# Head norm jobs at an even pace, their squares split in two parts, silu moved behind the z reload

## The reference, cut to what matters

```python
proj = xn @ w_in
gq = _l2norm(qkv[..., :GDN_WIDTH].reshape(B, L, GDN_HEADS, GDN_DK)) * (GDN_DK ** -0.5)
gk = _l2norm(qkv[..., GDN_WIDTH:2 * GDN_WIDTH].reshape(B, L, GDN_HEADS, GDN_DK))
z = proj[..., COL_GDN_Z:COL_GDN_B].reshape(B, L, GDN_HEADS, GDN_DV)
o_g = (_rmsnorm(o_g.astype(x.dtype), gdn_out_norm_g) * jax.nn.silu(z)).reshape(B, L, GDN_WIDTH)
dq = _rmsnorm(d[..., :DIFF_WIDTH].reshape(B, L, DIFF_HEADS, 2, DIFF_DQK), diff_q_norm_g)
dk = _rmsnorm(d[..., DIFF_WIDTH:2 * DIFF_WIDTH].reshape(B, L, DIFF_HEADS, 2, DIFF_DQK), diff_k_norm_g)
```

## Time and profile before

| what | us |
|---|---|
| median of 3 runs | 1883.97 (1883.55 to 1886.48) |
| the profiled execution, its own time | 1885.86 |
| its span, first to last instruction | 1884.3 |
| TensorE's matmuls, busy | 1728.3 (92%) |
| DVE, ACT, POOL, busy | 1018.8 (54%), 523.7 (28%), 248.3 (13%) |

### The profile page before, as it was taken

How to read it: one execution, slowest core, us unless ns; L and a number is a source line. 1 busy time by engine, 2 the same in 40 slices (tenths; PEclk the granted TensorE clock), 3 DMA queues, 4 the chain that set the end, 5 groups by cost and what they waited for, 6 DMA issues and landing times. The chain is left out here.

```text
span 1884.3 us, 28461 instructions
## 1 busy us (share of the span) xinstructions
PE 1728.3 (92%) x11078; PEld 1617.5 (86%) x11078; DVE 1018.8 (54%) x1469; ACT 523.7 (28%) x781; POOL 248.3 (13%) x434
## 2 busy tenths in 40 slices
PE   5999998897999999874768999999999999999998
PEld 5999977796888888752338999999999999999997
DVE  4444399942565556422263455555555655655654
ACT  4243332211344334301232232212212212212213
POOL 3100022203333333103100000000000000000000
PEclk9999999999899999956868999999999999999999
DMA  4311101022000000017422112101101101101103
GB/s 136 124 45 47 45 24 34 23 97 98 1 10 3 13 1 1 7 45 248 187 107 73 50 60 64 57 22 56 56 22 56 56 22 56 56 22 56 56 0 101
DMA packets 114550, 105.29 MB, mean 56 GB/s; under 512 B 5387, under 2 KB 104221, under 8 KB 112022
## 3 DMA queue, kind: packets, MB, share of 16 engines
q1 hardware_dynamic: 111666, 93.35, 16.0%
q0 software_dynamic: 1536, 8.39, 1.1%
q10 hardware_dynamic: 1270, 2.48, 0.4%
HBM read 86.13 MB, written 18.07 MB: 55 GB/s over the span
## 5 line engine op out<-in xcount | busy, mean ns | idle before, releaser
L2645 PE MATMUL f_up<-h_hi,w_hi 128*128 128x352 f32 x1032 | 335.1, 325 | 1.9 <-DVE w_lo L2454 1.2
L2645 PE MATMUL f_up<-h_hi,w_lo 128*128 128x352 f32 x1032 | 333.4, 323 | 0.0
L2645 PE MATMUL f_up<-h_lo,w_hi 128*128 128x352 f32 x1032 | 333.4, 323 | 0.0
L179 PE MATMUL proj<-x_hi,win_hi 128*128 128x352 f32 x672 | 227.5, 339 | 5.3 <-issue 3.0
L179 PE MATMUL proj<-x_hi,win_lo 128*128 128x352 f32 x672 | 217.9, 324 | 0.0
L179 PE MATMUL proj<-x_lo,win_hi 128*128 128x352 f32 x672 | 217.7, 324 | 0.0
L2645 PEld LDWEIGHTS f_up<-h_hi,w_hi 128*128 128x128 f32 x1032 | 193.8, 188 | 2.5 <-DVE w_lo L2454 1.5
L2645 PEld LDWEIGHTS f_up<-h_hi,w_lo 128*128 128x128 f32 x1032 | 194.1, 188 | 0.0
L2645 PEld LDWEIGHTS f_up<-h_lo,w_hi 128*128 128x128 f32 x1032 | 193.7, 188 | 0.0
L2652 PE MATMUL f_down<-f_g_hi,dn_hi 128*128 128x352 f32 x512 | 165.3, 323 | 0.0
L2652 PE MATMUL f_down<-f_g_hi,dn_lo 128*128 128x352 f32 x512 | 164.7, 322 | 0.0
(11 more groups left out here) (403 smaller groups left out, 3039.3 us busy)
## 6 DMA issues: line engine op xcount, KB each, us to landing
w_raw<-in_w_up SPq DMA_DIRECT2D x44, 512.0 KB, 3.9
win_raw<-in_w_in SPq DMA_DIRECT2D x28, 512.0 KB, 4.0
dn_raw<-in_w_down SPq DMA_DIRECT2D x11, 1024.0 KB, 5.2
p_key<-in_cache_k SPq DMA_DIRECT2D x32, 256.0 KB, 6.6
p_val<-in_cache_v POOLq DMA_DIRECT2D x32, 256.0 KB, 6.8
x_scratch<-feat SPq DMA_DIRECT2D x1, 4224.0 KB, 12.8
feat<-x_scratch SPq DMA_DIRECT2D x1, 4224.0 KB, 18.3
feat<-in_x_prompt SPq DMA_DIRECT2D x8, 512.0 KB, 9.0
```

Of the source, the lines that this page charges most:

```text
L179: mm = nc.tensor.matmul(out, w[:, k, :], x[:, k, g * TG:(g + 1) * TG], start=(k == 0 and i == 0), stop=(k == KT - 1 and i == 2))
L2645: mm = nc.tensor.matmul(up[u % RING][:, 0:TG], a[s][:, kk, :], b, start=(kk + x == 0), stop=(kk == KT - 1 and x == 2))
```

## The change

- Order of tiles: k, v, q, z (K0 = 12, V0 = 16, Q0 = 20, Z0 = 24). Order of jobs: delta-net q, attention k, delta-net k, attention q.
- The 48 jobs are spread over the 40 places from (14, 0) to (27, 0): one at each place, two at every fifth. Two stand at (15, 1), (17, 0), (18, 2), (20, 1), (22, 0), (23, 2), (25, 1) and (27, 0).
- The rows pieces start at (20, 1): two at each place to (21, 1), then one at (21, 2), none at (22, 0), and one at each place to (25, 0). ACT copies them out instead of DVE; they have two buffers, not three; SP stores the pieces of a tile between two weight loads. `bank` and `bank_is_free` give each use the other bank, and make it wait for the use before the last.
- The squares are split for fp32r: ACT rounds them (sq_hi), POOL makes the remainder (sq_lo, in the place of the squares), PE sums both with ones in fp32r: two passes of fp32r in place of one matmul in fp32.
- z goes to memory as it is, by two buffers. In head_gate ACT first waits for z and takes silu of its four tiles, then does what it did.
- The three tail turns stand all in tile 13, and small tensors share memory.

```diff
     def column(n):
+        if n < V0:
+            return COL_DIFF + GW + (n - K0) * P
         if n < Q0:
-            return COL_DIFF + GW + (n - K0) * P
-        if n < V0:
+            return COL_DIFF + 2 * GW + (n - V0) * P
+        if n < Z0:
             return COL_DIFF + (n - Q0) * P
...
     def jobs_in(n, g):
 
-        k = 3 * (n - K0 - 2) + g - 1
-        return range(max(0, 2 * k), min(NJ, 2 * k + 2))
+        k = NG * (n - K0 - 2) + g
+        return range(max(0, k * NJ // 40), max(0, min(NJ, (k + 1) * NJ // 40)))
 
     def pieces_in(n, g):
 
-        k = 3 * (n - Z0) + g
-        if k < 0:
-            return range(0)
-        first = 2 * k if k < 7 else 14 + (k - 7)
-        return range(first, min(NPIECE, first + (2 if k < 7 else 1)))
...
+        k = NG * (n - Q0) + g
+        if 1 <= k < 6:
+            return range(2 * k - 2, min(NT + 1, 2 * k))
+        if 7 <= k < NT + 8:
+            return range(NT + k - 6, NT + k - 5)
+        return range(0)
...
+    def bank_is_free(pe, kind, x):
+
+        u = uses.index((kind, x)) - 2
+        if u < 0:
+            pe.wait_ge(tail_rows, u + 4)
+        elif uses[u][0] == "job":
+            pe.wait_ge(sq_rooted, uses[u][1] + 1)
+        else:
+            pe.wait_ge(tok_kept, uses[u][1] + 1)
...
+                if n >= Q0 + 2:
+                    for g in range(NG):
+                        for p in pieces_in(n - 2, g):
+                            store_rows(sp, p)
...
+            def square_low(j):
+                pool.wait_ge(sq_hi_done, j + 1)
+                nc.gpsimd.tensor_tensor(sq_lo[j % 2][:, :], sq[j % 2][:, :], r32(sq_hi[j % 2][:, :]), ALU.subtract).then_inc(sq_lo_done, 1)
+
+            square(0)
             for j in range(NJ):
-                square(j)
+                if j + 1 < NJ:
+                    square(j + 1)
+                square_low(j)
...
+            def high_square(j):
+                act.wait_ge(sq_made, j + 1)
+                if j >= 2:
+                    act.wait_ge(sq_summed, j - 1)
+                nc.scalar.copy(sq_hi[j % 2][:, :], sq[j % 2][:, :]).then_inc(sq_hi_done, 1)
...
-                    nc.scalar.activation(z_buf[:, :].rearrange("p (g t) -> p g t", g=NG), psum[s][:, :, 0:TG],
-                                         ACT.Silu).then_inc(evacuated, 1)
...
+                    nc.scalar.copy(acc[s][:, 0:T].rearrange("p (g t) -> p g t", g=NG), psum[s][:, :, 0:TG]).then_inc(evacuated, 1)
...
                     for j in jobs_in(*at):
                         if j == 0:
                             act.wait_ge(eps_put, 2)
+                            high_square(0)
+                        if j + 1 < NJ:
+                            high_square(j + 1)
                         square_root(j)
+                    for p in pieces_in(*at):
+                        keep_rows(p)
...
-                pe.wait_ge(sq_made, j + 1)
-                nc.tensor.matmul(small[:, (j + 1) % 2, 0:TG], head_ones[:, e, :], sq[j % 2][:, :], start=True, stop=True
-                                 ).then_inc(sq_summed, 1)
+                bank_is_free(pe, "job", j)
+                pe.wait_ge(sq_lo_done, j + 1)
+                at = small[:, bank("job", j), 0:TG]
+                nc.tensor.matmul(at, head_ones[:, e, :], sq_hi[j % 2][:, :], start=True, stop=False)
+                nc.tensor.matmul(at, head_ones[:, e, :], sq_lo[j % 2][:, :], start=False, stop=True).then_inc(sq_summed, 1)
...
         @block.scalar
         def _(act):
+            act.wait_ge(z_in, 16)
+            for t in range(H):
+                nc.scalar.activation(zT[:, t, :], zT[:, t, :], ACT.Silu).then_inc(z_made, 1)
             n_act(act)
...
-            dve.wait_ge(z_in, 16)
+            dve.wait_ge(z_made, H)
```

More of the change, by code:

```diff
@@ L198, in norm_and_projection @@
     ba_w = m.sb("ba_w", [P, KT, 4 * H], F32R)
-    NTOK = 3
+    NTOK = 2
     tok = [m.sb(f"by_token{s}", [P, GW]) for s in range(NTOK)]
[L201 to L206, removed]
-    head_eps = m.sb("head_eps", [P, 2])
[L208 to L211, removed]
+    a_pos, a_neg = (tok[0][:, x * H * (NT + 1):(x + 1) * H * (NT + 1)].rearrange("p (t h) -> p t h", h=H) for x in range(2))
+    dt_bias, a_log = (tok[0][:, 128 + x * H:128 + (x + 1) * H] for x in range(2))
+    head_eps = m.sb("head_eps", [P, 2])
+    head_ones = m.sb("head_ones", [P, 2, P], F32R)
+    sq_hi = [m.sb(f"head_sq_hi{s}", [P, TG], F32R) for s in range(2)]
+    scale_at = m.take(4 * 4 * TG)
+    sq = [m.at(f"head_sq{s}", [P, TG], F32, scale_at + 4 * TG * s) for s in range(2)]
+    root = [m.at(f"head_root{s}", [P, TG], F32, scale_at + 4 * TG * (2 + s)) for s in range(2)]
+    sq_lo = [m.at(f"head_sq_lo{s}", [P, TG], F32R, scale_at + 4 * TG * s) for s in range(2)]
+    rows = m.at("rows", [20, P], F32, scale_at)
+    lam = m.at("lam", [P, 4, HALF], F32, scale_at + 4 * P)
+    diag = [m.at(f"x_diag{s}", [P, P], F32, scale_at + 4 * P * (3 + s)) for s in range(2)]
     lam_sum = m.sb("lam_sum", [P, 4])
@@ L250, in norm_and_projection @@
     pads = sem("g_pads")
-    z_out = sem("z_out")
+    z_out = [sem(f"z_out{s}") for s in range(2)]
     ba_loaded, ba_split, ba_projected, ba_kept, ba_turned, ba_put = (
@@ new lines, in pieces_in @@
+        if 1 <= k < 6:
[3 more added lines that the diff above has]
+        return range(0)
+    slots = [(n, g) for n in range(K0, NTILE) for g in range(NG)]
+    uses = [use for at in slots for use in [("job", j) for j in jobs_in(*at)] + [("rows", p) for p in pieces_in(*at)]]
+    assert [u for u in uses if u[0] == "job"] == [("job", j) for j in range(NJ)]
+    assert [u for u in uses if u[0] == "rows"] == [("rows", p) for p in range(NPIECE)]
@@ L516, in square_root, with keep_rows @@
                     act.wait_ge(normed, j - 1)
-                nc.scalar.activation(root[j % 2][:, :], small[:, (j + 1) % 2, 0:TG], ACT.Sqrt, bias=head_eps[:, e:e + 1], scale=1.0
+                nc.scalar.activation(root[j % 2][:, :], small[:, bank("job", j), 0:TG], ACT.Sqrt, bias=head_eps[:, e:e + 1], scale=1.0
                                      ).then_inc(sq_rooted, 1)
+            def keep_rows(p):
+                act.wait_ge(tok_turned, p + 1)
+                if p >= NTOK:
+                    act.wait_ge(tok_out[p % NTOK], 16 * (p // NTOK))
+                n = rows_of(p % (NT + 1))
+                nc.scalar.copy(tok[p % NTOK][0:n, :], small[0:n, bank("rows", p), :]).then_inc(tok_kept, 1)
             def gate_functions():
```

109 lines of the change are left out of this document (45 added, 64 removed).

## The result

| | before | after |
|---|---|---|
| median of the runs | 1883.76 us (4 runs, 1881.38 to 1886.48) | 1905.65 us (4 runs, 1900.78 to 1908.09) |
| the profiled execution's own time | 1885.86 us | 1908.09 us |
| its span | 1884.3 us | 1906.4 us |
| granted clock over the span | 0.952 | 0.938 |

The ratio is 1.0099, with a 95% interval of 1.008 to 1.0118: slower by 1%. The direction is the forecast's. The time is 10 us above its 1895.5, outside the forecast's own 1890 to 1902 and just inside the whole range of 1878 to 1906; of the cases written down, the first half of rival 4 (the clock) comes nearest.

A forecast was written before the change was run, and what follows sets the result against it. After the spread PE, no longer DVE, bounds tiles 12 to 27: 38.8 us freed less 30.0 waits and 7.4 clock, 1.4 gained; head_gate loses 13.0; net +11.6, 1883.97 becomes 1895.5. Own range 1890 to 1902, whole range 1878 to 1906.

The forecast's parts named there:

- rival 4: Tiles 12 to 27: clock falls behind all ten waits (17 for 7.4), or fp32r sums keep old price (+13); chance 0.10.
- What bounds the kernel: Tiles 12 to 27: DVE is full before; the even spread makes PE the bound and frees 38.8 us if PE never waits.
- pace of the fp32r sums: Job sums on PE: two fp32r passes take 0.32 us, 48 make 15.4; the old 0.6 a job would cost 13 us.
- Rival 5: Spreading fails: DVE stays the bound, tiles 12 to 27 stay at 254.7 us, net +13, 1897; chance 0.05.
- The waits: PE in tiles 12 to 27: six pairs 12.8, pairs at (18, 2) and (23, 2) 6.7, first job 6.1, pieces 4.4; 30.0 us.
- Rival 2: Tiles 12 to 27: PE hardly waits, the second job's low part being ready in time; net -12.8 us, 1871; chance 0.12.
- The clock: Tiles 12 to 27: 4.3 falls of the granted clock behind PE's waits, 1.7 us each, 7.4 us; bounds 1.7 and 17.
- Rival 1: Tiles 12 to 27: the clock stays up, with one fall or none; net +5.9 or +4.2 us, 1888 to 1890; chance 0.15.
- head_gate: Start of head_gate: ScalarE waits for z, four silus and a second table load, so squares start 13.0 us late; bounds 5.4 and 15.
- Rival 3: Start of head_gate: z lands after 5 us, not 8.8, so ScalarE starts 3.8 earlier; net +7.8, 1892; chance 0.06.
- The rule on GpSimd: Low parts in tiles 12 to 27: contention with DVE's scaling, hitting all sixteen passes, would add 9 us; most taken as not hit.
- a term put at nothing: Outside tiles 12 to 27 and head_gate's load: no change in time forecast, 0 us.

The follow-up runs named there:

- e6: Changed kernel with the squares summed whole in fp32, no high and low parts; 1880.02 us, 0.9971 of the kernel before.
- e3: Changed kernel with GpSimd making each job's low part right behind its square, ahead of the next job's square; 1891.96 us, 1.0026 of the kernel before.
- e1: Kernel before with only the silu moved: z stored as it is, head_gate takes its silus ahead of the squares; 1898.20 us, 1.0061 of the kernel before.
- e5: Changed kernel with e2, e3 and e4 together and the pairs at (18, 2) and (23, 2) moved one place on; 1863.76 us, 0.9893 of the kernel before.
- e8: The changed kernel run again for a second profile, nothing changed; 1906.50 us, 1.0107 of the kernel before.
- e2: Changed kernel with head_gate's silus put between its later squares; 1893.17 us, 1.0034 of the kernel before.
- e4: Changed kernel with ScalarE making the high parts of jobs 0 and 1 ahead of its gate functions; 1895.63 us, 1.0042 of the kernel before.
- e7: Changed kernel with the edits of e6 and e2 together; 1864.92 us, 0.9889 of the kernel before.

## Why the prediction came out 10 us low

**What bounds the kernel: right.** Once the jobs were spread, DVE's wait was gone and PE set the stretch. With the idle and lost time taken off, 218.8 us are left where 254.7 - 38.8 = 215.9 was forecast: 2.9 too few, half of it because a tile with three single jobs takes 12.51 and not 12.4. The disputed pace of the fp32r sums was rightly taken low: e6 shows the other format at 0.26 a sum more, and the 13 us of rival 4's second half did not come. Rival 5, that DVE stays the bound, fell with the 100 us of waits.

**The waits: right in kind, 4.1 too many.** 30.0 forecast, 25.9 measured. The first job 5.67 for 6.1; five pairs with 10.8 for six with 12.8 (the last pair has no further square of GpSimd ahead of it, and waits for nothing); the late pairs 6.6 for 6.7; the pieces 2.7 for 4.4, since 0.6 was put down three times and 0.21 came twice. Rival 2, that PE hardly waits, fell: 2.23 us stand before the second sum at (15, 1), and the square ahead of the low part is the reason (e3). Of the eight pairs only the last followed at once.

**The clock: the step that failed.** The prediction put 4.3 falls of 1.7, 7.4 us. There were seven and they cost 15.3: 7.9 of the missing 10. Two things were wrong in it. The chance of one in three came from two falls behind six waits of 2.00 us in one profile (e1, with the same six waits, has four), and was carried to waits that are 0.1 to 0.2 us longer, four of five of which had a fall here, and 17 of 21 in all profiles. And a fall behind a wait of 3.3 or 5.7 us is not the short one of the earlier trace rows: it lasts 6.8 us, begins inside the wait, and costs (15.3 - 4 x 1.7) / 3 = 2.8. Rival 1, that the clock stays up, fell. Rival 4 had "17 for 7.4" from ten falls of 1.7: near 15.3, but by the wrong count. That its 1905 is so close to the 1905.65 measured is luck, since waits and passes came out otherwise than it has them and 5.0 us lie elsewhere. Set against the forecast, the stretch is +7.9 for the clock, -4.1 for waits, +2.9 for the passes, 6.7 in all: from -1.4 to +5.3. That waits bring falls with them is shown by e5 and e6: with waits of 14.3 and 22.2 us gone, 13.7 and 15.3 of lost time went, where kernels with the same waits (after, e8 and e2) differ by no more than 3.5. The 2.9 of e4 are within that, and about half of e3's 10.7 lies at waits that it did not touch.

**head_gate: right.** 13.0 forecast, 11.8 measured, the difference being mostly z's landing, 7.8 for 8.8 us. ScalarE's idle time was to be 8.8 and is 6.50: the first table load stands inside the same landing, as the prediction's own sum had it. PE's sums behind it ran 0.75 us longer at the lower clock, inside the "up to 2" that was named. Rival 3, z landing after 5, fell. By the Trainium skill, ScalarE: Activation LUTs, section What ACT_TABLE_LOAD costs, a drain of 1.38 would come with each switch; the rows after a load in four kernels start 0.01 to 0.02 us behind it, so the trace does not bear that out.

**The rule on GpSimd.** The Trainium skill, GPSIMD Engine Reference, section Key points, has GpSimd contending with VectorE's instructions of two SBUF inputs. The trace agrees as far as it can show it: with DVE's scaling beside it the low pass at 260.04 took 1.21 us, where its shortest takes 0.923. It decided nothing: the pair waits came at up to 2.24, 0.1 above the sum with mean passes. The prediction's 9 us for it was too much even by its own terms: six pairs have twelve passes, and 12 x 0.55 is 6.6. And it works the other way too: that scaling took 0.94 where its shortest is 0.524.

**The other 5.0 us: a term put at nothing.** The prediction put down nothing outside the stretch and head_gate's load, and there the profiles differ by 1.8 + 1.8 + 1.4. No experiment was made for it, but the trace says what it is. These are the three parts, before and then after, and the first part in e8 (length, busy PE, PEld, DVE, ACT, POOL, granted clock, DMA):

```profile
0.00:195.51 195.51, 171.06 (x1095) 169.24 (x1096) 92.01 (x113) 75.91 (x120) 26.97 (x55) 0.98 0.28 87
450.19:937.25 487.06, 407.91 (x3006) 340.95 (x3006) 228.31 (x476) 147.05 (x341) 146.15 (x189) 0.87 0.14 50
938.54:1884.30 945.76, 911.42 (x5590) 890.23 (x5590) 520.12 (x731) 231.70 (x223) 32.82 (x137) 0.98 0.17 53
...
0.00:197.29 197.29, 173.37 (x1095) 171.55 (x1096) 92.38 (x113) 75.96 (x120) 27.00 (x55) 0.96 0.28 86
457.29:946.15 488.86, 410.76 (x3006) 344.69 (x3006) 228.01 (x476) 146.91 (x340) 146.40 (x188) 0.87 0.14 50
959.25:1906.40 947.15, 912.68 (x5590) 890.85 (x5590) 519.55 (x730) 231.70 (x223) 31.56 (x134) 0.98 0.16 48
...
0.00:195.57 195.57, 171.64 (x1095) 169.88 (x1096) 91.96 (x113) 75.90 (x121) 26.92 (x55) 0.98 0.28 87
```

TensorE has the same matmuls in each part, by their number, and works 2.3, 2.9 and 1.3 us longer at them, 6.4 in all; it sits idle for 1.4 less. That goes with the clock: 17.1 us at half clock in the first part for 6.8, 126.3 in the second for 122.9, 46.8 in the last for 44.4. The first part is the luck of one execution and not the change's: e8, the same kernel, has 6.8 at half clock there, and 195.57 us. In the other two e8 is longer than before as well (488.5 and 947.3), and whether the change brings that about stays open. So of the 10.5 us that the span is above the forecast's 11.6, 6.7 are the stretch, -1.2 head_gate's load and 5.0 this.

## What to carry to other kernels

When TensorE is made the bound, price each wait that is left at its length plus what the clock takes behind it; here that second part was 60% of the first, and no wait under 1.6 us had a fall put down to it in ten profiles. Splitting an operand for a cheaper matmul saves on TensorE, but the halves have to be made, and waits for them can eat the saving: here nearly all of it was eaten (e5 against e7). If you split, put the producer's passes in the order in which they are waited for, not the next item's first (e3). And an operation moved behind a load belongs where its engine already waits, here between the squares and not in front of them.

## What the runs showed of the hardware

All waits of TensorE of 0.2 us and more in this stretch, over the ten profiles, with a fall of the granted clock to 0.50 beside them:

| wait, us | waits | with a fall | at half clock each |
|---|---|---|---|
| 0.2 to 1.6 | all others | 0 | |
| 1.95 | 5 | 0 | |
| 2.00 to 2.07 | 13 | 6 | 3.4 |
| 2.13 to 2.24 | 21 | 17 | 3.4 |
| 3.32 | 10 | 8 | 6.8 (one 3.4) |
| 5.67 | 4 | 4 | 6.8 |

A fall is put down to the wait that it begins in, or that ended at most 1.9 us before it, and to the longer of two. The neighbours of a wait differ too, so this is what was seen beside it, not a law, and the length of a wait alone does not decide. The same kernel twice (after, e8) had its falls at the same seven places; but e2, whose code in this stretch is the same and whose waits agree to 0.02 us, had six, with none at the first wait of 3.32 and at the piece's 2.24, and one at the pair at (25, 1). The wait of 3.32 in e2, and the clock beside it:

```profile
310.45 0.40 PE L895 MATMUL proj_small<-head_sq_hi,head_ones 128*128 128x352 f32 x1 [3.32 <-POOL head_sq_lo L435]
...
309.00:311.00 2.00, 0.55 (x3) 0.58 (x4) 1.46 (x2) 1.13 (x3) 0.93 (x1) 1.00 0.28 36
```

So what the clock costs over one set of waits varied between 11.9 and 15.4 us in three profiles. Unexpected too: GpSimd's pass that writes fp32r from two inputs has a median of 0.948 us where the square of the same shape has 0.775, and none of the 48 is under 0.923, so the second pass is not to be priced as the first. Operation, inputs and output format all differ between the two, and no run here tells which of them costs the 0.17.
